# Two transformer blocks in one program: first attention with scores overwritten by their exponentials, its second V product moved, normalisation and last scaling shared by two engines

## The reference

```python
def first_block(x, c, ctx, c_ctx, w_ada, ...):
        mod_x = (silu_c @ w_ada[i] + b_ada[i])[:, None, :]
        ...
        hx = modulate(rms_norm(x, norm1_g[i]), sh1, sc1)
        hc = modulate(rms_norm(ctx, norm1_g[i]), csh1, csc1)
        qx, kx, vx, ux = split_proj(hx @ w_in[i])
        kvc = hc @ w_in[i][:, ATT_DIM:3 * ATT_DIM]          # keys and values of the context
        qx_rot = axial_rope(qx, row_pos, col_pos)
        kx_rot = axial_rope(kx, row_pos, col_pos)
        attn_x = neighbourhood_attention(qx_rot, qx, kx_rot, vx, kc, vc, rpb[i])
        conv_x = conformer_conv(ux, dw_kernel[i], dw_bias[i], conv_ln_g[i], conv_ln_b[i])
        x_new = x + g1 * (jnp.concatenate([attn_x, conv_x], axis=-1) @ w_out[i])
        ...
# attention of one head: 256 window scores (with bias, masked by it) beside 256 context scores
        p = jax.nn.softmax(jnp.concatenate([s_win, s_ctx], axis=-1), axis=-1)
        out = p_win @ v + p_ctx @ v_ctx
# convolution: 31 taps over tokens, per channel, then layer norm over 512 channels and silu
def second_block(...):
    ...
    x = x + (jax.nn.silu(h @ w_gate[layer]) * (h @ w_up[layer])) @ w_down[layer]
    return rmsnorm(x, norm_final)
```

## Time and profile before

| | |
|---|---|
| median of 3 runs | 769.57 us (767.3 to 772.62) |
| the profiled execution | 769.86 us, of which the span of the trace is 767.7 us |
| TensorE busy | 735.3 us, 96% of the span |
| VectorE busy | 491.7 us, 64% |
| ScalarE busy | 386.5 us, 50% |
| mean granted TensorE clock | 0.991 of full speed |
| HBM read | 143.22 MB, 188 GB/s over the span |

### The profile page before, as it was taken

How to read it: one execution, slowest core, us unless ns; L and a number is a source line. 1 busy time by engine, 2 the same in 40 slices (tenths; PEclk the granted TensorE clock), 3 DMA queues, 4 the chain that set the end, 5 groups by cost and what they waited for, 6 DMA issues and landing times.

```text
span 767.7 us, 9561 instructions
## 1 busy us (share of the span) xinstructions
PE 735.3 (96%) x3764; PEld 578.4 (75%) x3764; DVE 491.7 (64%) x878; ACT 386.5 (50%) x635; POOL 23.6 (3%) x44
## 2 busy tenths in 40 slices
PE   4999998899999999999989999999999999999996
PEld 2668885556878888888868777777788888888885
DVE  3468999975575544535679979964857645455443
ACT  3356225756475454544564567658255544343431
POOL 1002001100000000000010000000000000000000
PEclk9899999999999999999999999999999999999999
DMA  9994839853654545654346634435544666555511
GB/s 321 368 333 172 316 123 327 277 167 107 219 191 166 213 151 185 219 188 151 119 155 222 224 127 165 148 110 152 177 135 149 214 203 208 189 183 201 165 55 56
DMA packets 80844, 144.89 MB, mean 189 GB/s; under 512 B 4048, under 2 KB 35792, under 8 KB 80800
## 3 DMA queue, kind: packets, MB, share of 16 engines
q1 hardware_dynamic: 79136, 139.24, 52.9%
q0 software_dynamic: 1520, 5.03, 1.9%
q10 hardware_dynamic: 144, 0.01, 0.0%
HBM read 143.22 MB, written 1.05 MB: 188 GB/s over the span
## 4 chain that ended last, share of the span: by engine, by line
PE 75%; DVE 15%; ACT 3%; issue 2%; DMA 2%; SPq 1%; POOL 0%; DVEq 0%; POOLq 0%; ACTq 0%
PE bank L405 22%; PE bank L407 21%; PE bank L406 21%; DVE cacc L1396 5%; PE bank L387 4%; DVE WL L1381 4%; DMA WX<-in_w_ada 2%; PE bank L424 1%; ACT WH L952 1%; DVE X L1390 1%; PE bank L806 1%; PE bank L828 1%; PE bank L447 1%; DVE s L1558 1%; DMA W<-in_w_mlp 1%
## 5 line engine op out<-in xcount | busy, mean ns | idle before, releaser
L1381 DVE TENSOR_TENSOR WL<-W,WH 128x1024 fp32r<-128x1024 f32 (+1 forms) x214 | 248.0, 1207 | 56.3 <-ACT WH L952 55.4
L405 PE MATMUL bank<-WH,AH 128*128 128x512 f32 (+1 forms) x608 | 243.2, 400 | 5.6 <-DVE WL L1381 3.9
L407 PE MATMUL bank<-WH,AL 128*128 128x512 f32 (+1 forms) x608 | 236.0, 388 | 0.0
L406 PE MATMUL bank<-WL,AH 128*128 128x512 f32 (+1 forms) x608 | 235.9, 388 | 0.0
L952 ACT ACTIVATE WH<-W 128x1024 fp32r<-128x1024 f32 (+1 forms) x214 | 210.0, 1041 | 15.9 <-DMA W<-in_w_in 5.8
L405 PEld LDWEIGHTS bank<-WH,AH 128*128 128x128 f32 x608 | 114.5, 188 | 38.2 <-issue 10.5
L407 PEld LDWEIGHTS bank<-WH,AL 128*128 128x128 f32 x608 | 114.5, 188 | 24.4
L406 PEld LDWEIGHTS bank<-WL,AH 128*128 128x128 f32 x608 | 114.7, 189 | 21.3 <-issue 0.2
L405 PE MATMUL bank<-WH,HH 128*128 128x512 f32 x216 | 84.7, 392 | 0.0
L407 PE MATMUL bank<-WH,HL 128*128 128x512 f32 x216 | 84.2, 390 | 0.0
L406 PE MATMUL bank<-WL,HH 128*128 128x512 f32 x216 | 84.1, 389 | 0.0
(11 more groups left out here) (230 smaller groups left out, 694.8 us busy)
## 6 DMA issues: line engine op xcount, KB each, us to landing
W<-in_w_mlp SPq DMA_DIRECT2D x32, 1024.0 KB, 5.5
W<-in_w_in SPq DMA_DIRECT2D x28, 1024.0 KB, 5.7
W<-in_w_ada SPq DMA_DIRECT2D x12, 1024.0 KB, 6.6
WX<-in_w_ada SPq DMA_DIRECT2D x12, 1024.0 KB, 9.6
W<-in_w_gate SPq DMA_DIRECT2D x22, 512.0 KB, 3.9
W<-in_w_up SPq DMA_DIRECT2D x22, 512.0 KB, 5.3
W<-in_w_down SPq DMA_DIRECT2D x11, 1024.0 KB, 5.0
W<-in_w_out SPq DMA_DIRECT2D x8, 1024.0 KB, 5.0
```

Of the source, the lines that this page charges most:

```text
L405: e.matmul(po, hs, wh[:, k, c0:c0 + cw], start=first and k == 0, stop=False)
L406: e.matmul(po, hs, wl[:, k, c0:c0 + cw], start=False, stop=False)
L407: ins = e.matmul(po, ls, wh[:, k, c0:c0 + cw], start=False, stop=last and k == unit.nk - 1)
L1381: e.tensor_tensor(m.WL[unit.slot][:, c], m.W32[unit.slot][:, c], m.WH[unit.slot][:, c].bitcast(F32), ALU.subtract).then_inc(S["w_lo"], 1)
```

## The change

Seven edits in the code, told by place:

- **Head.** ScalarE splits weight unit ab1 ahead of `modulate_odd(1)` and ab3 ahead of `modulate_odd(3)`. VectorE calls `lo()` for ab1, ab2, ab3 ahead of `modulation(1)`, `(2)`, `(3)` instead of behind `low_quarter`.
- **Context features.** The transposed context is scaled and shifted straight from its bank; the copy to `hTc` before it is gone on both engines.
- **Rotation.** `rope1` rotates both token tiles in one call (6 instructions where there were 12), for k and for q; it waits for both tiles' copies.
- **Second V product.** v of the second token tile goes to bank 5 and is moved behind all of `qk_turn`, with `scores1(0)` between its halves. `soft1` no longer waits for it. ScalarE copies it out behind the first two exponentials.
- **Attention buffers.** The scores have six buffers instead of four, the exponential overwrites them, `P1` is gone. `soft1(n)` now waits for `turn1(n - 6)`, `exp1` for its maximum alone, and ScalarE takes `exp1` one step ahead. Of the two rows of a step VectorE scales the even one and ScalarE the odd one. `norm1` stands first in the step on VectorE; taps are spread anew: 52 before the loop instead of 54, then 4, and 8, 10, 3, 3, 12 in steps 0 to 4.
- **Convolution sums.** They go to the second half of bank 5 instead of banks 6 and 7, and stand ahead of `pv1(u - 1)`; `ccen` lies where `s1` was.
- **End.** The last product of the second token tile is written as 512, 256 and 256 columns to banks 1, 4, 5; the sums of squares are taken in three parts; of the second tile's output VectorE scales the first half and ScalarE the second, and ScalarE issues that half's transfer.

```diff
...
-        self.P1 = [M(f"P1_{i}", 48 + 2 * i, [128, 512]) for i in range(2)]
         self.PT1 = [M(f"PT1_{i}", 52 + 2 * i, [128, 512]) for i in range(2)]
-        self.s1 = [M(f"s1_{i}", (28, 30, 60, 62)[i], [128, 512]) for i in range(4)]
+        self.s1 = [M(f"s1_{i}", (68, 70, 60, 62, 48, 50)[i], [128, 512]) for i in range(6)]
...
-        frees(b, ("hc_act" if i % 2 else "hc_dve", i // 2 + 1))
+        frees(b, ("mc_act" if i % 2 else "mc_dve", 3 * (i // 2) + 2))
...
     product(by["v"], m.AH, m.AL, 0, 0, "v_mm", x_ready)
+    frees(0, ("v_out", 1))
     qk_turn(m.KC, 0, "kc_out")
     qk_turn(m.Q, 1, "q_out")
-    product(by["v"], m.AH, m.AL, 1, 1, "v_mm", x_ready)
-    for tb in range(2):
-        frees(tb, ("v_out", tb + 1))
-    qk_turn(m.KR, 2, "kr")
-    qk_turn(m.QR, 3, "qr")
+    qk_turn(m.KR, 2, "kr", 1)
+    qk_turn(m.QR, 3, "qr", 1)
...
-        w.wait_ge(S["p1_norm"], n + 1)
-        b = turn(four(m.P1[n % 2]), "p1_turned")
+        w.wait_ge(S["p1_norm_act" if n % 2 else "p1_norm"], n // 2 + 1)
+        b = turn(four(m.s1[n % 6]), "p1_turned")
...
-        frees(5, ("o1_lo", u + 1))
+        frees(5, ("o1_lo", u + 1), *conv_reads)
+        conv_reads.clear()
...
+    product(by["v"], m.AH, m.AL, 1, 5, "v_mm", x_ready, 512, lambda: scores1(0))
+    frees(5, ("v_out", 2))
     for u in range(8):
         if u < 7:
             scores1(u + 1)
         mod_second(2 * u)
         if u:
             mod_second_tail(u - 1)
-            pv1(u - 1)
         if u == 5:
             conv_mean()
         if u == 6:
             conv_var()
         if u == 7:
             conv_spread()
+        if u:
+            pv1(u - 1)
...
+    def down2_last():
+
+        for n, (c0, cw) in enumerate(LAST[1]):
+            part(by["dn", 10][0], m.HH[0], m.HL[0], 0, 1, (1, 4, 5)[n], n > 0, True, "dn_mm",
+                 lambda k: ("hid_lo", 38), c0, cw)
+
...
     copy(two(m.hT, 3), bank[m.turn_bank["x_turned", 4]][:, :], "hx_act")
+    hi()
     modulate_odd(1, m.hT, m.AH, 0, "x")
     hi(2)
     modulate_odd(3, m.hT, m.AH, 0, "x")
-    hi(3)
+    hi(2)
...
         w.wait_ge(S["max1"], n + 1)
-        if n > 1:
-            w.wait_ge(S["p1_turned"], n - 1)
-        e.activation(m.P1[n % 2][:, :], m.s1[n % 4][:, :], ACT.Exp, bias=m.mneg[:, n:n + 1], scale=-1.0,
+        e.activation(m.s1[n % 6][:, :], m.s1[n % 6][:, :], ACT.Exp, bias=m.mneg[:, n:n + 1], scale=-1.0,
                      accum_out=m.lsum[:, n:n + 1]).then_inc(S["exp1"], 1)
...
+    def norm1(u):
+
+        w.wait_ge(S["rl1"], u + 1)
+        n = 2 * u + 1
+        copy(m.s1[n % 6][:, :], m.s1[n % 6][:, :], "p1_norm_act", m.rl[:, n:n + 1])
+
...
+    exp1(0)
+    exp1(1)
+    from_bank("v_mm", 8, m.V[:, 1, :], 5, slice(0, 512), "v_out")
     for u in range(8):
-        exp1(2 * u)
-        exp1(2 * u + 1)
+        norm1(u)
+        if u < 7:
+            exp1(2 * u + 2)
+            exp1(2 * u + 3)
...
+    w.wait_ge(S["rstd"], 14)
+    w.wait_ge(S["x_g"], 1)
+    copy(m.S1[:, 1, 512:1024], m.S1[:, 1, 512:1024], "y_act", m.stat[:, 53:54])
+    w.wait_ge(S["y_act"], 1)
+    e.dma_start(out[128:256, 512:1024], m.S1[:, 1, 512:1024]).then_inc(S["l_out"], 16)
...
     for i in range(4):
         rows_out(i)
+        if i:
+            lo()
         modulation(i)
         if i % 2 == 0:
             modulate_even(i, m.hT, m.AH, 0, "x")
         low_quarter(i, m.hT, m.AH, m.AL, "x")
-        lo()
         if i == 0:
+            lo()
             x_features(2)
...
+    def rope1(dst, src, sem):
+
+        def heads(t):
+            return t[:, :, :].rearrange("p t (h e) -> p t h e", e=64)
+
+        def table(i, x, n):
+            return m.rope1[:, :, i, x:x + n].unsqueeze(2).to_broadcast([128, 2, 8, n])
+
+        tt(heads(dst), heads(src), table(0, 0, 64), ALU.mult, "rope_mul")
+        mul["n"] += 1
+        for at in (0, 32):
+            for x, y in ((at, at + 16), (at + 16, at)):
+                tt(heads(m.tmp)[:, :, :, x:x + 16], heads(src)[:, :, :, y:y + 16], table(1, x, 16), ALU.mult, "rope_mul")
+                mul["n"] += 1
+        w.wait_ge(S["rope_mul"], mul["n"])
+        tt(dst[:, :, :], dst[:, :, :], m.tmp[:, :, :], ALU.add, sem)
+
     w.wait_ge(S["l_first"], 48)
     w.wait_ge(S["kc"], 4)
-    for tb in range(2):
-        w.wait_ge(S["k_out"], tb + 1)
-        if tb:
-            w.wait_ge(S["kr"], 1)
-        rope(m.KR[:, tb, :], m.Kt[:, tb, :], 8, m.rope1, 16, tb, "kr")
+    w.wait_ge(S["k_out"], 2)
...
-        if n > 3:
-            w.wait_ge(S["exp1"], n - 3)
-        e.tensor_tensor_reduce(out=m.s1[n % 4][:, :], in0=m.bias[h % 4][:, tb, :], in1=bank[SCORE1_BANKS[tb][j]][:, :], scale=-1.0,
+        if n > 5:
+            w.wait_ge(S["p1_turned"], n - 5)
...
-        for n in (2 * u, 2 * u + 1):
-            times(m.P1[n % 2][:, :], m.P1[n % 2][:, :], m.rl[:, n:n + 1], "p1_norm")
+        n = 2 * u
+        times(m.s1[n % 6][:, :], m.s1[n % 6][:, :], m.rl[:, n:n + 1], "p1_norm")
...
     soft1(0)
     soft1(1)
+    taps(4)
     for u in range(8):
+        norm1(u)
         if u < 7:
             soft1(2 * u + 2)
             soft1(2 * u + 3)
-        taps(2)
         if u:
+            taps(2)
             mod_second_tail(u - 1)
-        norm1(u)
-        taps(6)
+        taps((8, 8, 1, 1, 10, 0, 0, 0)[u])
         if u:
             o1_lo(u - 1)
...
+        if tb:
+            w.wait_ge(S["dn_mm"], DN_AT[9, 1])
+            tt(m.X[:, 1, 512:1024], bank[3][:, :], m.X[:, 1, 512:1024], ALU.add, "res3")
+        for n, (c0, cw) in enumerate(LAST[tb]):
+            w.wait_ge(S["dn_mm"], DN_AT[10, tb] - 1 + n)
+            if tb and n:
+                w.wait_ge(S["res3"], 3)
+            bk = ((0, 2), (1, 4, 5))[tb][n]
+            tt(m.X[:, tb, c0:c0 + cw], bank[bk][:, 0:cw], m.X[:, tb, c0:c0 + cw], ALU.add, "res3")
...
+    w.wait_ge(S["res3"], 6)
+    tt(m.S1[:, 1, 512:1024], m.X[:, 1, 512:1024], m.g2b[:, 512:1024], ALU.mult, "x_g")
+    w.wait_ge(S["sq_sum"], 24)
+    e.tensor_scalar(col(39), col(22), col(23), EPS, ALU.add, ALU.add).then_inc(S["last_sum"], 1)
+    w.wait_ge(S["last_sum"], 1)
+    w.wait_ge(S["sq_sum"], 25)
+    tt(col(37), col(38), col(39), ALU.add, "mean_sq")
+    final(1, 0)
...```

How the change moves instructions, at three places. Names are those of the program with their buffer numbers; `x4` is four alike in a row; a line of "..." leaves rows out.

TensorE between the transposes of q and the first transposes of the attention. Before (`bank1` takes v of the second token tile, `P1` the first exponentials):

```order
L387 MATMUL bank6<-ident_80,Q_108 128x128 x4
L387 MATMUL bank7<-ident_80,Q_108 128x128 x4
L405 MATMUL bank1<-WH_0_61,AH_96 128x512
...
L407 MATMUL bank1<-WH_1_62,AL_97 128x512
L387 MATMUL bank6<-ident_80,KR_121 128x128 x4
...
L387 MATMUL bank7<-ident_80,QR_120 128x128 x4
L561 MATMUL bank0<-kT_124,qrT_122 128x256
...
L424 MATMUL bank4<-WX_2_69,csp_100 32x512 x4
L387 MATMUL bank6<-ident_80,P1_0_131 128x128 x4
```

135 lines of the change are left out of this document (66 added, 69 removed).

## The result

The changed kernel takes **759.02 us** (median of 4 runs, 758.15 to 760.28), the kernel before 769.28 us (4 runs, 767.30 to 772.62): ratio **0.9864**, 95% interval 0.9825 to 0.9902, some 10.3 us or 1.3% faster. Forecast were 759.9 us and a range of 756 to 765. The profiled execution has a span of 757.9 us, 9.8 less than before. The sum came out; its terms did not all, and most of this document is about that. Executions of one kernel differ with the granted clock: spans of 756.3 to 758.4 us (mean clock 0.995 and 0.991) for the changed kernel here, and over 18 executions measured later 764.1 to 770.0 us (0.998 and 0.989) for the kernel before. Quickest against quickest the change is worth some 7.8 us, so part of the 10.3 comes and goes with the clock.

A forecast was written before the change was run, and what follows sets the result against it. The prediction took TensorE's own work plus its waits to bound the kernel. Head 1.9, attention 7.3 and end 0.8 summed to 10.0 us off 769.9, so 759.9 us, with an 8-in-10 range of 756 to 765.

The forecast's parts named there:

- Head: Before the attention: TensorE resumes on ab3 near 48.8 us instead of 50.65, held by late features, not weights; gain 1.9 us.
- Rival 1: In the head, ab1 and ab3 land later and hold the features back; total 761.8 to 765.5 us, chance 0.10.
- VectorE arrives in time: At the attention's start: the first transposes find their data; moving the V product counts zero beyond the wait it covers.
- The three waits for `P`: Attention loop: TensorE's three waits for scaled exponentials from VectorE all go; gain 4.4 us.
- The two waits for the centred convolution: Attention loop: two waits from banks shared by sums and transposes go with the sums in bank 5; gain 2.2 us.
- `conv_var`: Attention loop: standing ahead of `pv1`, it waits for the squares; loss 0.6 us, between zero and 1.1.
- Clock: At 126 us in the attention: without 1.9 us of idle the clock has no such reason to fall; gain 1.6 us.
- Rival 3: At eight groups of transposes in a row the clock falls earlier, slowing half the V product; total 762.2 us, chance 0.07.
- rival 4: The lower clock level stays through the attention loop, slower than before; over all 52 us 783 us, chance 0.04.
- GpSimd's power: Step 7 of the loop: `conv_spread` waits for the power, beside which a VectorE scaling runs; loss 0.3 us, 0 to 1.0.
- rival 2: Attention loop: ScalarE takes VectorE's place and TensorE waits for it, 3.6 us come back; total 763.4 us, chance 0.12.
- End: Last output: half the columns in the last add and two output halves made side by side; gain 0.8 us, bounds 0 and 1.2.

The follow-up runs named there:

- v_back: Changed kernel with the second V product back between the transposes of Q and of the rotated K; median 760.2 us, 0.9886 of the kernel before.
- norm_dve: Changed kernel with all 16 scalings of exponentials back on VectorE, two a step, none on ScalarE; median 758.6 us, 0.9869 of the kernel before.
- same_step: Changed kernel with exponentials no longer taken one step ahead and the next two maxima before the reciprocal; median 760.5 us, 0.9890 of the kernel before.
- centre_first: Changed kernel; in step 5 VectorE centres the convolution ahead of its weight subtractions, ScalarE squares it ahead of its weight splits; median 757.4 us, ratio 0.9855.
- best: centre_first plus the second half of ab3's low part behind the modulation and VectorE's last output half sent in two pieces; median 756.1 us, ratio 0.9838.
- head_old: Changed kernel with the head's order of the kernel before on ScalarE and VectorE; median 761.3 us, 0.9914 of the kernel before.
- loop_old: Changed kernel with VectorE's and ScalarE's loop order of the kernel before, both scalings on VectorE; moved V product, six buffers, bank 5 sums stay; median 764.0 us.
- loop_v_old: loop_old with the second V product also back between the transposes; median 764.1 us, 0.9931 of the kernel before.
- centre_dve: Changed kernel with only VectorE centring the convolution ahead of its weight subtractions, ScalarE still squaring behind its splits; median 759.2 us, ratio 0.9876.

## Why the prediction was right, and where it was wrong

**Head: right in kind, too small.** Said: resume at 48.8, features late, not weights, gain 1.9. Measured: 48.29, features late, gain 2.7. Two things were missed. A late low part is waited for twice, once for each half: 0.74 and then 0.3 us in the matmuls of ab1, so that VectorE's copy came 1.3 us earlier (43.74 to 42.43), not 0.7. And the gain hangs on the early clock fall, which the changed head absorbs and the old one doesn't. The distance that the prediction gives as 2.8 us is 2.9 by its own rows (46.08 to 49.02), and 2.9 after (45.30 to 48.24). The landing of ab3, estimated at 42.3, was 41.89. Rival 1 did not come, but close: that landing is what now bounds the head in executions without the early fall.

**VectorE arrives in time: right**, and v_back shows that it would have been 0.86 late otherwise. "The move counted at zero" missed that the wait for `qrT`, 0.74, goes while only some tenths come back: the waits of that stretch fell from 1.5 to 1.1 us.

**The three waits for `P`, 4.4 us: right**, and the reason given too simple. The prediction credits the reciprocal's place, the exponentials a step ahead and the shared scalings. norm_dve says the last is not needed while the others stand; same_step costs 0.7 alone, and the taps, which the prediction did not credit in the loop, cost 1.0; all of it undone costs 4.4, with a further shift of the reciprocal that was not tried alone.

**The two waits for the centred convolution, 2.2 us: right** as removed waits; kept in the new loop they would have cost 3.4. **`conv_var`: 0.46**, forecast 0.6.

**Clock, 1.6 us: this step failed.** "Without the 1.9 us of idle before them the clock has no such reason to fall" is borne out at 126 us (no profile of the changed kernel or its variants has a fall there), but a fall came at 160, behind the new wait ahead of 16 one-column products; that the wait is its reason is supported by seven of ten against none of four, not proven. "Granted clock 1.00 through the loop" holds in the profiles of centre_first and best, not in the profiled execution of the changed kernel. I had priced `conv_var`'s wait by its own length and not by the fall that it can bring, which costs more than three times as much. Rival 3, an earlier fall, had the right kind and the wrong place; rival 4 did not come: every profiled fall in the loop ended after some 3.6 us.

**GpSimd's power, 0.3: nothing.** GpSimd after:

```profile
163.42 0.72 POOL L342 TENSOR_TENSOR cvar<-cvar,stat 128x2 f32<-128x2 f32 x1 [29.64 <-DVE cvar L1633]
```

0.72 us beside VectorE's scaling (163.45, 0.48 us), and 0.72 in the kernel before, where no scaling ran beside it. By the rows the power began 0.03 us ahead of the scaling, the two overlapped, and neither got longer. By the exclusive lock of the Trainium skill ("SBUF — State Buffer", "SBUF: two separate sides"), which the one that starts first holds for its whole instruction, one of the two would have had to wait; these rows don't show it, though spans on GpSimd are rough. In norm_dve, with two scalings in a row, the power took 0.94; TensorE did not wait for it there either.

**ScalarE: right.** No wait for `PT` or `rows2`, and in a step with a weight split ScalarE still idles 0.38 us; rival 2 did not come. Relieving it (norm_dve) gains nothing.

**End, 0.8: wrong, 0.1.** The engines' part was 0.9, close to the 0.8 worked out. What stood behind it, the landing, I had left out of the term, as if it stayed at 2.0 us; with both halves ready at once it is 2.8.

**Sum.** Head +0.8; attention -0.4, of which clock -1.6, power +0.3, `conv_var` +0.1, `qrT` +0.4, and +0.3 or +0.4 that no wait row shows; end -0.7; the rest +0.1: together -0.2 us. Errors of up to 1.6 us cancelled, and that is luck: the total was right by more than its terms deserved. The reading of the waits, which carried 6.6 of 10 us, was sound.

## What to carry to other kernels

Where a stretch is bound by waits of an engine that others feed, price the waits and not the edits: of three edits that looked like three gains, each partly covered for the others, and one of them could have been left out. Undoing them one at a time showed 1.7 us of 4.4; most of the rest showed only when they were undone together. A gain made just ahead of the last transfers, or just ahead of a landing, has to be priced with the transfers. And a wait of half a microsecond ahead of small matmuls can come with a fall of the clock: look first for an order in which the feeding engine serves it earlier, which here was one exchange of two pieces of work on each of two engines and gave 2.3 us in the profiles, 1.7 in the medians, at no cost.

## What the runs showed of the hardware

- The clock falls in some executions and not in others. Much the same instructions had a granted clock of about 0.5 from 17 to 24 us in four profiled executions, for a shorter time in four, and not at all in six (head_old, norm_dve, loop_old, loop_v_old, centre_dve, best); behind a wait of 1.72 us in the head it fell in head_old and not in the kernel before; behind 1.95 us in the loop it fell, behind 1.76, 1.52 and 1.28 it did not. Single runs of one kernel differ by up to 6.0 us (766.26 to 772.23, the kernel before), the longer ones at the lower mean clock (0.989 against 0.998). The Trainium skill ("TensorE: Matmul & The Clock Gate", "Why this matters for your kernels") ties a drop in the middle of a kernel to long idle gaps between bursts of matmuls; here a fall came behind a gap of only 0.46 us ahead of small ones in seven profiled executions of ten.
- A stretch that waits anyway can be indifferent to it: with the changed head the context's transposes start within 0.2 us of each other, early fall or not.
- Two transfers of 256 KB issued together from two queues took 2.6 and 2.8 us to land; 0.7 us apart from one queue, 2.0 each.
